# Weights straight from memory by GpSimd: which ring slots are staged, and by whose queue they are loaded

## The reference

```python
def expert_block(args):                       # a block of rows of one expert
    xb, e = args
    gu = xb @ w_up[e] + b_up[e]               # 1024 x 2048 weights
    gate, up = gu[:, :D_EXPERT], gu[:, D_EXPERT:]
    gate = jnp.minimum(gate, SWIGLU_LIMIT)
    up = jnp.clip(up, -SWIGLU_LIMIT, SWIGLU_LIMIT)
    act = (up + 1.0) * (gate * jax.nn.sigmoid(SWIGLU_ALPHA * gate))
    return act @ w_down[e] + b_down[e]        # 1024 x 1024 weights
```

## Time and profile before

| | |
|---|---|
| time, median of 3 runs | 1282.32 us (1281.82 to 1283.32) |
| time of the profiled execution | 1281.05 us |
| span of the profiled execution | 1279.3 us |
| PE, DVE, ACT, POOL busy | 1154.7, 530.1, 242.8, 603.7 us |
| bytes moved, mean rate | 449.03 MB, 351 GB/s |

### The profile page before, as it was taken

One profiled execution on the slowest core, in us unless ns is written; L12 is line 12 of the kernel. 1 busy time (PEld: TensorE's weight loads), 2 busy tenths in 40 slices (PEclk: granted clock), 3 DMA queues, 4 the chain that ended last, 5 costly groups with the idle time before them and its releaser, 6 DMA issues.

```text
span 1279.3 us, 30496 instructions
## 1 busy us (share of the span) xinstructions
PE 1154.7 (90%) x11113; PEld 585.1 (46%) x11114; DVE 530.1 (41%) x1161; ACT 242.8 (19%) x483; POOL 603.7 (47%) x647
## 2 busy tenths in 40 slices
PE   8999999999999899799788997987988889789694
PEld 7777777775444334243233443433433334234242
DVE  2999984122633424333232442333323223423333
ACT  2012124001122222122112221211221212122122
POOL 0022300000556738547661586575565657638561
PEclk9999999999999999999899998999998899989998
DMA  8994433741999999999998899999999999999994
GB/s 244 325 303 130 142 131 109 285 178 68 378 397 401 407 422 422 422 422 421 422 422 369 326 393 423 422 421 422 422 422 422 422 422 422 422 422 422 422 422 173
DMA packets 94577, 449.03 MB, mean 351 GB/s; under 512 B 8526, under 2 KB 42894, under 8 KB 45339
## 3 DMA queue, kind: packets, MB, share of 16 engines
q1 hardware_dynamic: 93742, 446.55, 87.1%
q10 hardware_dynamic: 749, 1.19, 0.3%
q0 software_dynamic: 48, 0.85, 0.2%
HBM read 447.00 MB, written 2.42 MB: 351 GB/s over the span
## 4 chain that ended last, share of the span: by engine, by line
PE 63%; DMA 20%; DVE 14%; issue 1%; ACT 1%; POOL 0%; SPq 0%; DVEq 0%; ACTq 0%; POOLq 0%
PE banks L1387 23%; DMA ring<-in_w_down 19%; PE banks L1397 14%; DVE arena L810 8%; PE banks L1185 8%; PE banks L1100 5%; PE banks L1165 4%; PE banks L1137 3%; PE banks L1301 2%; PE banks L1174 2%; PE banks L1144 2%; DMA arena<-in_w_up 1%; DVE arena L819 1%; DVE arena L822 0%; PE banks L1270 0%
## 5 line engine op out<-in xcount | busy, mean ns | idle before, releaser
L539 POOL COPY ring<-arena 128x1024 f32<-128x1024 f32 x279 | 292.1, 1047 | 439.1 <-POOLq L536 373.9
L1387 PE MATMUL banks<-ring,hT 128*32 128x512 f32 x3328 | 419.0, 611 | 44.0 <-POOL ring L541 32.7
L541 POOL COPY ring<-arena 128x1024 f32<-128x1024 f32 x279 | 292.3, 1048 | 36.7 <-POOL ring L539 0.9
L1397 PE MATMUL banks<-ring,hT 128*32 128x256 f32 x3328 | 235.0, 404 | 52.0 <-DMA ring<-in_w_down 52.0
L334 DVE TENSOR_TENSOR xq<-xq,banks 128x256 f32<-128x256 f32 x53 | 22.3, 421 | 553.8 <-PE banks L1174 553.8
L1397 PEld LDWEIGHTS banks<-ring,hT 128*32 128x32 f32 x3328 | 105.8, 115 | 200.0 <-issue 92.6
L1387 PEld LDWEIGHTS banks<-ring,hT 128*32 128x32 f32 x3328 | 104.2, 112 | 192.1 <-issue 119.8
L1185 PE MATMUL banks<-hT,ring 128*128 128x288 f32 x768 | 188.4, 406 | 0.3 <-ACT hT L564 0.3
L1185 PEld LDWEIGHTS banks<-hT,ring 128*128 128x128 f32 x768 | 145.1, 190 | 39.7 <-issue 0.4
L810 DVE SCALAR_TENSOR_TENSOR arena<-arena 128x256 f32<-128x256 f32 x240 | 108.1, 528 | 0.0
L681 ACT COPY WT<-banks 128x256 f32<-128x256 f32 x52 | 19.4, 373 | 410.3 <-PE banks L1397 410.3
(11 more groups left out here) (249 smaller groups left out, 759.2 us busy)
## 6 DMA issues: line engine op xcount, KB each, us to landing
arena<-in_w_up SPq DMA_DIRECT2D x248, 1024.0 KB, 17.8
ring<-in_w_down SPq DMA_DIRECT2D x97, 1024.0 KB, 11.9
arena<-in_w_down SPq DMA_DIRECT2D x31, 1024.0 KB, 18.5
ring<-in_w_in SPq DMA_DIRECT2D x24, 1024.0 KB, 11.5
ring<-in_w_up SPq DMA_DIRECT2D x8, 1024.0 KB, 4.8
ring<-in_w_branch_b SPq DMA_DIRECT2D x4, 1024.0 KB, 4.8
ring<-in_w_branch_a SPq DMA_DIRECT2D x4, 1024.0 KB, 4.8
ring<-in_w_out SPq DMA_DIRECT2D x4, 1024.0 KB, 4.9
```

The source lines that it names most:

```text
L539: nc.gpsimd.tensor_copy(ring[:, k, 0:D], parked[k][:, 0:D]).then_inc(half_copied, 1)
L541: nc.gpsimd.tensor_copy(ring[:, k, D:SLOT], parked[k][:, D:SLOT]).then_inc(slot_full[k], 16)
L1387: ins = mm(UP[g * BLK:(g + 1) * BLK, :], xT[:, k, :], ring[:, k, g * 512:(g + 1) * 512], start=k == 0, stop=k == UP_SLOTS - 1)
L1397: ins = mm(DN[q * BLK:(q + 1) * BLK, 0:256], actT[:, f % 4, f // 4, :], ring[:, UP_SLOTS + j, h * D + q * 256:h * D + (q + 1) * 256], star ...
```

## The change

Which slots are staged is altered, and who loads the others. Staged are now slots 1 to 8 and 11 (`STAGED`); direct are 0, 9 and 10 (`DIRECT`). The direct loads are issued by POOL and not by SP, in POOL's own order of turns (`TURNS`): direct 0, copies 1 to 7, direct 9, copy 8, direct 10, copy 11. SP's loop over experts issues the nine staged loads only and waits for nothing but their copies. PE waits for a direct slot on a semaphore of its own (`direct_full`). For the first expert too, slots 0, 9 and 10 are loaded by POOL.

```diff
+STAGED = [1, 2, 3, 4, 5, 6, 7, 8, 11]
+DIRECT = [0, 9, 10]
+TURNS = [0, 1, 2, 3, 4, 5, 6, 7, 9, 8, 10, 11]
...
+        direct_full = [sem(f"direct_full{k}") for k in DIRECT]
...
             def load_parked(e, k):
 
-                sp.dma_start(parked[k], weights(e, k)).then_inc(parked_full[k], 16)
-
-            def load_direct(e, before, ks):
-
-                for k in ks:
-                    sp.wait_ge(down_used, before * DOWN_SLOTS + (k - UP_SLOTS + 1))
-                    load_slot(e, k)
+                n = STAGED.index(k)
+                sp.dma_start(parked[n], weights(e, k)).then_inc(parked_full[n], 16)
...
-            def next_weights(place, here, after, before):
-
-                load_parked_again(place + 1, after, range(UP_SLOTS - 2))
-                load_direct(here, before, range(PARKED, SLOTS))
-                load_parked_again(place + 1, after, range(UP_SLOTS - 2, PARKED))
-
             with sp.Fori(1, NE - 1) as place:
-                before = sp.value_load(items_before[0:1, bass.ds(place - 1, 1)], min_val=0, max_val=MAX_ITEMS)
-                here = sp.value_load(order[0:1, bass.ds(place, 1)], min_val=0, max_val=NE - 1)
                 after = sp.value_load(order[0:1, bass.ds(place + 1, 1)], min_val=0, max_val=NE - 1)
-                next_weights(place, here, after, before)
-            before = sp.value_load(items_before[0:1, NE - 2:NE - 1], min_val=0, max_val=MAX_ITEMS)
-            here = sp.value_load(order[0:1, NE - 1:NE], min_val=0, max_val=NE - 1)
-            load_direct(here, before, range(PARKED, SLOTS))
+                load_parked_again(place + 1, after, STAGED)
...
+            def wait_used(before, k, turn):
+
+                if k < UP_SLOTS:
+                    pool.wait_ge(up_used, before * UP_SLOTS + (k + 1))
+                else:
+                    pool.wait_ge(down_used, before * DOWN_SLOTS + (k - UP_SLOTS + 1))
+                pool.sem_inc(slot_free, 1)
+                pool.wait_ge(slot_free, turn + 1)
+
+            def copy_slot(e, k, n):
+
+                pool.wait_ge(parked_full[n], 16 * e)
+                nc.gpsimd.tensor_copy(ring[:, k, 0:D], parked[n][:, 0:D]).then_inc(half_copied, 1)
+                pool.wait_ge(half_copied, (e - 1) * PARKED + n + 1)
+                nc.gpsimd.tensor_copy(ring[:, k, D:SLOT], parked[n][:, D:SLOT]).then_inc(slot_full[k], 16)
+
+            def load_slot(e, k):
+
+                pool.dma_start(ring[:, k, :], weights(e, k)).then_inc(direct_full[DIRECT.index(k)], 16)
+
+            for k in DIRECT:
+                pool.wait_ge(*mix_block_used(MIX_BLOCKS - SLOTS + k))
+                load_slot(0, k)
             pool.wait_ge(before_known, 1)
             for e in range(1, NE):
                 before = pool.value_load(items_before[0:1, e - 1:e], min_val=0, max_val=MAX_ITEMS)
+                here = pool.value_load(order[0:1, e:e + 1], min_val=0, max_val=NE - 1)
+                for n, k in enumerate(TURNS):
+                    wait_used(before, k, (e - 1) * SLOTS + n)
+                    if k in STAGED:
+                        copy_slot(e, k, STAGED.index(k))
                     else:
+                        load_slot(here, k)
...
+            def wait_full(k, fills):
+
+                if k in STAGED:
+                    pe.wait_ge(slot_full[k], fills)
+                else:
+                    pe.wait_ge(direct_full[DIRECT.index(k)], fills - 16 * FILLS)
```

More of the change, by code:

```diff
@@ L313, in root, with weights @@
                                  ).then_inc(done, 1)
+        def weights(e, k):
+            if k < UP_SLOTS:
+                return a["w_up"][0, bass.ds(e, 1), k * P:(k + 1) * P, :].rearrange("e p n -> (e p) n")
+            j = k - UP_SLOTS
+            return a["w_down"][0, bass.ds(e, 1), j * 256:(j + 1) * 256, :].rearrange("e (p h) n -> p (e h n)", p=P)
         def load_root_table():
@@ L390, in _ @@
                 load_block(n)
[L392 to L397, removed]
             def load_slot(e, k):
@@ L420, in _ @@
             sp.wait_ge(v_stored, 16)
-            for k in range(EARLY_SLOTS):
+            for k in STAGED[:EARLY_SLOTS]:
                 load_parked(1, k)
-            for k in range(UP_SLOTS):
+            for k in range(1, UP_SLOTS):
                 sp.wait_ge(*mix_block_used(MIX_BLOCKS - SLOTS + k))
@@ L426, in _ @@
                 if k == 3:
-                    load_parked(1, EARLY_SLOTS)
+                    load_parked(1, STAGED[EARLY_SLOTS])
             sp.wait_ge(ya_evac, 2 * KC)
-            for k in range(EARLY_SLOTS + 1, PARKED - 1):
+            for k in STAGED[EARLY_SLOTS + 1:PARKED - 1]:
                 load_parked(1, k)
-            for k in range(UP_SLOTS, SLOTS):
+            for k in (UP_SLOTS, SLOTS - 1):
                 sp.wait_ge(*mix_block_used(MIX_BLOCKS - SLOTS + k))
                 load_slot(0, k)
-            load_parked(1, PARKED - 1)
+            load_parked(1, STAGED[PARKED - 1])
             sp.wait_ge(before_known, 1)
-            def next_weights(place, here, after, before):
-                load_parked_again(place + 1, after, range(UP_SLOTS - 2))
-                load_direct(here, before, range(PARKED, SLOTS))
-                load_parked_again(place + 1, after, range(UP_SLOTS - 2, PARKED))
             with sp.Fori(1, NE - 1) as place:
-                before = sp.value_load(items_before[0:1, bass.ds(place - 1, 1)], min_val=0, max_val=MAX_ITEMS)
-                here = sp.value_load(order[0:1, bass.ds(place, 1)], min_val=0, max_val=NE - 1)
                 after = sp.value_load(order[0:1, bass.ds(place + 1, 1)], min_val=0, max_val=NE - 1)
-                next_weights(place, here, after, before)
-            before = sp.value_load(items_before[0:1, NE - 2:NE - 1], min_val=0, max_val=MAX_ITEMS)
-            here = sp.value_load(order[0:1, NE - 1:NE], min_val=0, max_val=NE - 1)
-            load_direct(here, before, range(PARKED, SLOTS))
+                load_parked_again(place + 1, after, STAGED)
             for tt in range(NT):
@@ L530, in _ @@
                 before = pool.value_load(items_before[0:1, e - 1:e], min_val=0, max_val=MAX_ITEMS)
-                for k in range(PARKED):
-                    if k < UP_SLOTS:
-                        pool.wait_ge(up_used, before * UP_SLOTS + (k + 1))
-                    else:
[L535 to L541, removed]
+                here = pool.value_load(order[0:1, e:e + 1], min_val=0, max_val=NE - 1)
[3 more added lines that the diff above has]
+                        copy_slot(e, k, STAGED.index(k))
+                    else:
+                        load_slot(here, k)
         @block.scalar
@@ L1381, in _ @@
             mm(bank[6][:, 0:2 * NE], ones[0:NE, :], placed, start=True, stop=True).then_inc(order_summed, 1)
+            def wait_full(k, fills):
[3 more added lines that the diff above has]
+                    pe.wait_ge(direct_full[DIRECT.index(k)], fills - 16 * FILLS)
             def up(k, fills):
-                pe.wait_ge(slot_full[k], fills)
+                wait_full(k, fills)
                 for g in range(4):
@@ L1391, in down @@
             def down(j, fills):
-                pe.wait_ge(slot_full[UP_SLOTS + j], fills)
+                wait_full(UP_SLOTS + j, fills)
                 for h in range(2):
```

## The result

| | before | after |
|---|---|---|
| time, median of 4 runs | 1282.82 us | 1298.85 us (1298.70 to 1299.97) |
| span of the profiled execution | 1279.3 us | 1298.3 us |

The ratio is 1.0128, 95% interval 1.011 to 1.0145: 16.0 us slower. The forecast was 1267 us, faster; it was wrong in sign.

The account below looks back on a forecast made before the run. The DMA stream at 422 GB/s was taken as the bound. 1281.05 us profiled, less 12.9 (hole near 700 us) and 2.5 (early lead), is 1265.7; with 1.3 for the median, 1267 us, range 1260 to 1290.

Parts of the forecast that it names:

- What bounds the kernel: DMA engines at 422 GB/s: 954 us for 384 loads against 811 us of PE work, so PE's idle time there costs nothing.
- The early lead, 2.5 us: Before 420 us: two more staged loads asked for early, worth between 0 and 5.0 us; the middle, 2.5, was taken.
- The hole near 700 us, 12.9 us: After 420 us, behind the three-item expert: the DMA engines would no longer run out of work, gaining 12.9 us.
- PE can finish that step at 662: Step for expert number 12: weights up to slot 7 fetched by 659 us, so PE finishes that step at 662.
- Slot 0: Behind each one-item expert, the now direct load comes late: 11 PE stalls of 6.7 us, 74 us, within 100 us idle.
- my own point of 11.4 us: Landing time of slot 0's direct load at which PE's 100 us of idle time no longer covers the stalls.
- The end, taken as 0 with 2 us as the other end: Last expert: slots 9 and 10 asked for behind copy 7, costing 0, at most 2 us.
- GpSimd, hidden: Per expert, POOL's copies and three issues take 21.6 to 26.1 us against 29.8 us of DMA, so cost nothing.
- The rate, 0: A quarter of the remaining bytes through the software queue: no loss, far end 62 us; rival of a lower rate 0.17.
- The rule of two slow engines: Skill's rule: two of sixteen DMA engines usually slower with software-written descriptors, so the stream would stand below 422 GB/s.
- GpSimd's issue: Time POOL spends issuing one direct load: 0.74 us as measured for 48 packets, up to 2.2 us for 144.
- the second, a late slot 0: Rival, chance 0.16: landing nearer 17.8 than 9 us, PE stalls up to 15 us, holes return; 1276 to 1288 us.

Follow-up runs that it names:

- e1: Changed kernel with direct slots 9, 10, 11 as before the change, still issued by GpSimd, and slot 0 staged again: 1290.15 us, ratio 1.0063.
- e6: e2 with only the last expert's slot 0 asked for earlier, ahead of the `down` turns of the expert before: 1281.45 us, ratio 0.9992.
- e11: e6 with GpSimd taking all twelve turns, waiting and making two small copies at those of slots 0, 9 and 10: 1287.14 us, ratio 1.0038.
- e12: e11 without the small copies, so GpSimd only waits at the turns of slots 0, 9 and 10: 1283.85 us, ratio 1.0007.
- e5: Changed kernel with only the last expert's slot 0 asked for earlier, ahead of the `down` turns of the expert before: 1287.30 us, ratio 1.0033.
- e4: Changed kernel with slot 11 direct in place of slot 10, which is staged: 1309.47 us, ratio 1.0205.
- e8: e2 with only slot 0's loads put through GpSimd's queue, 9 and 10 staying in SyncE's: 1295.91 us, ratio 1.0104.
- e3: Changed kernel with the first two turns swapped, so slot 0 is asked for one copy later: 1299.01 us, ratio 1.0124.
- e2: Changed kernel's slots, but SyncE issues all loads in the order of the turns and GpSimd only copies: 1292.73 us, ratio 1.0079.

## Why the prediction was wrong

**What bounds the kernel.** Right: 422 GB/s bound the middle. Ten waits of PE with 107.5 us in all left it 9.5 us late at item 50, and from 770 to 1220 us the stream lost 3.8 us. The cover isn't free of a condition, though: it holds while the store takes what the stream brings, and the next term fails by that.

**The early lead, 2.5 us.** It was made (7.9 us lost by the stream before 420 us became 3.8) and given back: what was lost between 690 and 770 us went from 13.5 to 17.7.

**The hole near 700 us, 12.9 us.** Wrong, and the step that failed is "PE can finish that step at 662": it finished at 687. The bytes were there: from 413 to 661 us are 100 loads, 153 MB with the 53 at the start. PE was not. The timeline of the changed kernel:

```profile
659.57 0.53 POOL L534 DMA_DIRECT2D ring<-in_w_up  x1 [0.85 <-POOLq L522]
...
673.16 6.24 PE L1401 MATMUL banks<-ring,hT 128*32 128x512 f32 x32 [12.21 <-DMA ring<-in_w_up]
...
685.93 1.04 PE L1401 MATMUL banks<-ring,hT 128*32 128x512 f32 x8
...
708.69 0.53 POOL L534 DMA_DIRECT2D ring<-in_w_up  x1 [19.78 <-POOLq L522]
```

Slot 0 of that expert was asked for at 659.6 and read at 673.2, when the other up slots had long landed. I had PE at the expert's last item at 683 us; GpSimd's wait for slot 0 of the next ended at 708.7. PE so starts an item when its last part has come rather than its first. The store is that much fuller, and the expert with three items fills it as before. I had removed one cause of PE's lateness and put another, slot 0, in its place. This is read from the trace of the changed kernel, and slot 0 is not the only way to the hole: e1 has no wait for it and still loses 15.3 us from 690 to 770. Over all kernels here the loss in that stretch is 13.5 to 17.8 us. None closed it, so what would have is open.

**Slot 0.** Forecast eleven waits of 6.7 us, covered by 100 us of idle time. Measured eleven of 10.9 us, 119.6 us. The landing was 9.6 us in the median of all, near my 9, but in the eleven waits 10.1 to 13.6 us from issue to PE's first step, 12.6 in the median, most likely because slot 10's load stood in the same queue. That is over my own point of 11.4 us. In the middle the cover held all the same, measured against the kernel before: e6 keeps such waits, 101 us, and equals it. Measured against my forecast it did not, since the 12.9 us were never gained. At the end it did not hold at all.

**The end, taken as 0 with 2 us as the other end.** This is the largest part of the loss. I followed slots 9 and 10 there and not slot 0, though I had worked out its wait for "each" expert of one item and the last pair are two such. With nothing staged for a next expert, the wait runs the stream dry, and the loads that only PE's steps release come behind it. Measured: 11.3 and 11.6 us.

**GpSimd, hidden.** Wrong by 5.7 us (e11 less e6). My test was whether 26 us of work fit into 29.8. They do: GpSimd was busy 50% of the span. What costs is that its turns come in order: e12 adds waits alone and no work, and is 2.4 us above e6. That the copies behind such a turn are late is how I read it; the busy share doesn't show it.

**The rate, 0.** Right for this kernel, as far as e5 against e11 can tell: the software queue's 101.5 MB took 19.3% of the span, 405 GB/s of their own time, and the other queue's 345.88 MB took 66.8%, 399 GB/s. In e4 a lower rate does stand, unexplained. My 333 GB/s for a single transfer came from a share printed as 0.2%, too coarse for such a figure. The rule of two slow engines (the Trainium skill, DMA: Bandwidth & Descriptors, Latency and other measured facts) doesn't show in the total of the changed kernel; single engines are not in these views.

**GpSimd's issue.** 96 issues took 527 ns in the median and 628 at most, with VectorE busy 40% of the span. That is under both of my figures. The 3.1 us of the Trainium skill (SBUF — State Buffer, A bandwidth-pool intuition that's wrong) don't show in this kernel.

The sum as the runs have it: e6 stands at -1.0 us to the kernel before, GpSimd's turns add 5.7, the queue 0.2, the last slot 0 11.6: 16.5, against 16.0 measured. The forecast had -15.4 in place of these. So of its miss of 32 us some 14 are the gain in the middle that did not come, 11.6 the last slot 0 and 5.7 GpSimd's turns. Of my rivals the second, a late slot 0, came nearest; I had priced it in the middle only, at the time of the kernel before, and so without the end. The 5.7 us are in none of them.

## What to carry to other kernels

Where a stream of loads bounds a stretch, waits of the engine that uses it can be nearly free in the middle, as long as there is room for what the stream brings, and are dear at the end: follow the last round by itself, load by load, and ask for each what is queued behind it when nothing else is left to fetch. A load or a copy put on an engine that takes its turns in order is only as early as the latest wait ahead of it; count the waits of each turn for the shortest case (here an expert with one item), not the engine's busy time. A lead gained ahead of a point at which the store is full anyway was worth nothing here.

## What the runs showed of the hardware that I had not expected

In GpSimd's queue a load landed the later the closer ahead another had been issued. From slot 0's issue to PE's first step the median of eleven waits was 9.5 us with no other loads in GpSimd's queue (e8), 10.7 with one issued 5.3 us ahead (e3), 12.6 with one 3.6 us ahead (the changed kernel) and 12.9 with one 1.9 us ahead (e4). In SyncE's queue, with all other loads in it, it was 9.6 (e2), so this isn't a rule for every queue. Asking for it 1.5 us later (e3) made 0.6 us. Over all loads, those from GpSimd's queue landed as fast as those beside them in SyncE's (9.4 and 9.6 against 10.9 us) and cost GpSimd 0.53 us each, less than the 0.74 us of its one transfer of fewer packets. And a wait of PE costs more than its length. Behind the wait of 12.1 us at 1260.75 the granted clock had fallen to 0.50, the lower level, and the next 32 matmuls took 5.99 us against 3.64.
